# First RWKV layer's opening: two low-rank factors mixed ahead of the normed input, first weight splits issued in another place

## The reference

```python
h = rms_norm(x, norm_mix[0])
shifted = pad(h, one token)[:-1]
xm = h[:, :, None] + (shifted - h)[:, :, None] * mix      # six mixed inputs
r, k, v = xm[..., 0] @ w_r, xm[..., 1] @ w_k, xm[..., 2] @ w_v
logw = -softplus(-(w0 + tanh(xw @ w1) @ w2)) - 0.5        # xw = xm[..., 3], w1: 1024 x 64
decay = exp(-exp(logw))
a = sigmoid(a0 + (xa @ a1) @ a2)                          # xa = xm[..., 4], a1: 1024 x 64
g = sigmoid(xg @ g1) @ g2                                 # xg = xm[..., 5], g1: 1024 x 160
```

## Time and profile before

| | us |
|---|---|
| median of 3 runs | 1954.19 (1952.05 to 1954.6) |
| the profiled execution | 1962.87 |
| its span | 1960.7 |
| PE busy | 1834.4 (94%) |
| DVE busy | 1261.0 (64%) |
| ACT busy | 1043.6 (53%) |
| mean granted clock of PE | 0.967 |

### The profile page before, as it was taken

How to read it: one execution, slowest core, us unless ns; L and a number is a source line. 1 busy time by engine, 2 the same in 40 slices (tenths; PEclk the granted TensorE clock), 3 DMA queues, 4 the chain that set the end, 5 groups by cost and what they waited for, 6 DMA issues and landing times.

```text
span 1960.7 us, 43143 instructions
## 1 busy us (share of the span) xinstructions
PE 1834.4 (94%) x18559; PEld 1634.7 (83%) x18559; DVE 1261.0 (64%) x1783; ACT 1043.6 (53%) x1585; POOL 147.2 (8%) x106
## 2 busy tenths in 40 slices
PE   6988899999989999899899999988999999998998
PEld 5887798889869878888588888877788888887887
DVE  6865367865336666477657856777277766775764
ACT  5734455555455545355555555834455544565455
POOL 0061100000000000113100000052100000000000
PEclk8999999999989999999899999999999999998999
DMA  6320245557466655444646563320145555443541
GB/s 192 130 81 4 67 145 186 184 189 248 152 214 190 205 167 185 133 148 155 194 137 210 185 193 108 108 81 25 40 147 186 190 190 162 143 138 100 166 130 65
DMA packets 288532, 287.87 MB, mean 147 GB/s; under 512 B 15240, under 2 KB 286456, under 8 KB 288344
## 3 DMA queue, kind: packets, MB, share of 16 engines
q1 hardware_dynamic: 285048, 284.01, 45.4%
q10 hardware_dynamic: 3296, 1.11, 0.3%
HBM read 284.06 MB, written 1.05 MB: 145 GB/s over the span
## 4 chain that ended last, share of the span: by engine, by line
PE 89%; ACT 3%; DVE 3%; issue 3%; DMA 1%; POOL 0%; ACTq 0%; DVEq 0%; POOLq 0%
PE ps L419 22%; PE ps L420 12%; PE ps L401 10%; PE ps L402 9%; PE ps L403 9%; PE ps L814 3%; PE ps L436 2%; PE ps L437 2%; PE ps L438 2%; PE ps L712 1%; PE ps L784 1%; PE ps L675 1%; PE ps L798 1%; PE ps L641 1%; PE ps L676 1%
## 5 line engine op out<-in xcount | busy, mean ns | idle before, releaser
L463 DVE TENSOR_TENSOR wl<-raw,wh 128x1024 fp32r<-128x1024 f32 x484 | 597.2, 1252 | 366.0 <-ACT wh L453 361.7
L453 ACT ACTIVATE wh<-raw 128x1024 fp32r<-128x1024 f32 x484 | 499.5, 1041 | 452.8 <-PE ps L420 197.9
L419 PE MATMUL ps<-HH,wh 128*128 128x512 f32 x1408 | 491.2, 392 | 4.5 <-DVE mod L2143 4.5
L420 PE MATMUL ps<-HH,wl 128*128 128x256 f32 x1408 | 397.5, 282 | 0.0
L419 PEld LDWEIGHTS ps<-HH,wh 128*128 128x128 f32 x1408 | 265.0, 188 | 61.1 <-DVE mod L2143 4.8
L401 PE MATMUL ps<-HH,wh 128*128 128x256 f32 x928 | 272.8, 294 | 10.8 <-DVE HH L2511 5.7
L420 PEld LDWEIGHTS ps<-HH,wl 128*128 128x128 f32 x1408 | 266.7, 189 | 0.1
L402 PE MATMUL ps<-HH,wh 128*128 128x256 f32 x928 | 265.3, 286 | 0.0
L403 PE MATMUL ps<-HH,wl 128*128 128x256 f32 x928 | 265.1, 286 | 0.0
L401 PEld LDWEIGHTS ps<-HH,wh 128*128 128x128 f32 x928 | 181.0, 195 | 22.5 <-issue 6.8
L402 PEld LDWEIGHTS ps<-HH,wh 128*128 128x128 f32 x928 | 181.1, 195 | 1.3 <-issue 1.2
(11 more groups left out here) (324 smaller groups left out, 3138.3 us busy)
## 6 DMA issues: line engine op xcount, KB each, us to landing
raw<-in_ffn_w_gu_dram SPq DMA_DIRECT2D x88, 1024.0 KB, 5.1
raw<-in_ffn_w_down_dram SPq DMA_DIRECT2D x32, 1024.0 KB, 5.2
raw<-in_w_in_dram SPq DMA_DIRECT2D x32, 1024.0 KB, 5.5
raw<-in_rw_w_rkv_dram SPq DMA_DIRECT2D x24, 1024.0 KB, 5.6
B<-in_w_ada_dram SPq DMA_DIRECT2D x24, 1024.0 KB, 7.4
raw<-in_ds_w_in_dram SPq DMA_DIRECT2D x14, 1024.0 KB, 5.2
raw<-in_ffn_w_down_dram SPq DMA_DIRECT2D x16, 768.0 KB, 4.5
raw<-in_sb_w_qkv_dram SPq DMA_DIRECT2D x12, 1024.0 KB, 6.0
```

The source lines that it names most:

```text
L419: e.matmul(o[:, m, :], h_[:, k, c], x_, start=k0 + k == 0, stop=False, skip_group_check=True)
L420: i = e.matmul(o[:, m, 0:S], l_[:, k, c], x_[:, 0, :], start=False, stop=k0 + k == kt - 1, skip_group_check=True)
L453: e.activation(wh[:, u % UNITS, 0:kn * 256], raw[:, j % RAW, k0 * 256:(k0 + kn) * 256], ACT.Copy).then_inc(*up("hi"))
L463: e.tensor_tensor(wl[:, u % UNITS, 0:kn * 256], raw[:, j % RAW, k0 * 256:(k0 + kn) * 256], wh[:, u % UNITS, 0:kn * 256].bitcast(F32), ALU. ...
```

## The change

Four edits, all for the first RWKV layer alone (n == 0) but for the semaphore:

- The load of g1 gets a semaphore of its own, so that parts 3 and 4 wait for w1 and a1 alone.
- DVE mixes parts 3 and 4 before it waits for `rstd` and makes `h`; part 5 stays behind `h`.
- ACT makes `hi` of units 0 and 1 only, then waits for "wa" and takes tanh and copy, then does `prepare(1)`'s roundings, then `hi` of units 2 and 3, then `prepare(0)`'s.
- DVE makes `lo` of units 0 to 3 between `prepare(1)` and `prepare(0)`, and of units 4 and 5 ahead of the scan; the last `lo` before the fourth new key goes.

```diff
-            for name, a, z in (("rw_w1", 0, 64), ("rw_a1", 64, 128), ("rw_g1", 128, 256)):
-                e.dma_start(down[:, :, a:z], wview(A[name][n])[:, :, 0:z - a]).then_inc(s_down, 16)
+            for name, a, z, landed_ in (("rw_w1", 0, 64, s_down), ("rw_a1", 64, 128, s_down), ("rw_g1", 128, 256, s_down_g)):
+                e.dma_start(down[:, :, a:z], wview(A[name][n])[:, :, 0:z - a]).then_inc(landed_, 16)
...
-            hi(e, 2 if n else 4)
-            prepare(1, HH)
+            hi(e)
+            if n:
+                prepare(1, HH)
             e.wait_ge(*at("mm", ("wa", n)))
             e.activation(lor[0:64, :], PS("wa", n)[0:64, 0:S], ACT.Tanh)
             e.activation(lor[64:128, :], PS("wa", n)[64:128, 0:S], ACT.Copy).then_inc(*up("act", ("wa", n)))
+            if n == 0:
+                prepare(1, HH)
+                hi(e)
             prepare(0, XH)
...
-            e.wait_ge(s_down, 48 * (n + 1))
             for m in parts:
+                if m == 5:
+                    e.wait_ge(s_down_g, 16 * (n + 1))
+                else:
+                    e.wait_ge(s_down, 32 * (n + 1))
...
+            if n == 0:
+                dve_lora(e, 0, 3, 4)
             e.wait_ge(*at("act", (("rms w", n), "rstd")))
...
             if n == 0:
-                dve_lora(e, 0, 3, 4, 5)
+                dve_lora(e, 0, 5)
...
             prepare(1, (HH, HL))
+            if n == 0:
+                lo(e, 4)
             prepare(0, (XH, XL), ("dve", ("xml", n, 1, 3)))
-            lo(e, 2 if n else 4)
+            lo(e)
...
             if n == 0:
                 dve_lora_tail(e, 0)
                 dve_late_rows(e)
-            lo(e)
+            else:
+                lo(e)
             new_key(3)
```

More of the change, by code:

```diff
@@ L173, in build @@
         s_rows = [sem(f"s_rows{i}") for i in range(3)]
-        s_down, s_tail, s_lora_up, s_v2 = (sem(f"s_{n}") for n in ("down", "tail", "lora_up", "v2"))
+        s_down, s_down_g, s_tail, s_lora_up, s_v2 = (sem(f"s_{n}") for n in ("down", "down_g", "tail", "lora_up", "v2"))
         def C(name, a=0, b=None):
```

## The result

| | before | changed |
|---|---|---|
| median of 12 runs, us | 1960.36 (1952.05 to 1970.53) | 1968.37 (1960.55 to 1972.13) |
| ratio, 95% interval | | 1.0040 [1.0023, 1.0058] |
| profiled execution (span), us | 1962.87 (1960.7) | 1971.44 (1969.3) |
| granted clock, mean | 0.967 | 0.967 |
| chain of the span: PE, DVE, ACT | 89%, 3%, 3% | 86%, 5%, 4% |

The account below looks back on a forecast made before the run. PE was taken to bound the kernel, with little slack on DVE and ACT. Terms 2.65 + 2.5 + 2.7 = 7.9 us, taken as +8 on the median 1954.19, gave 1962.2 us; range 1956.5 to 1967.

Parts of the forecast that it names:

- the last line of the sum: Whole kernel: +8 us, giving 1970.9 against the profiled 1962.87, or 1962.2 against the median 1954.19.
- Part 1: DVE's factors ahead of h: they cost nothing in an idle gap, and PE begins "wa" 5.8 us earlier.
- Part 2: ACT waits for "wa" ahead of the roundings: first rounding into HH 1.67 us late, all of prepare(1) queued behind.
- my lower bound: Opening: the clock never falls, "wa" takes 6.9 us, the 1.67 us and the clock term vanish; +3.7 us.
- Part 3: Four `lo` between the inputs delay the sigmoid freeing "g"'s bank; PE's fourth w2/a2 group waits until 42.95: +2.65 us.
- Part 4: PE's clock after its 8.4 us stop: 0.50 for 5.1 us, until 48.0, delaying the first key unit: +2.5 us.
- Part 5: `lo` of units 4 and 5 ahead of DVE's scan: PE stands 2.7 us before the key's fourth block: +2.7 us.
- more clock loss: Rival: clock at 0.50 until 26.2 and again after the second stop; +12.4 us, 1966.6; chance 0.15.
- the early start: Rival: PE's opening starts 5.8 us earlier and nothing takes it back; 1948.4, faster; chance 0.05.
- the clock did cost: Judges the rival of no clock loss in PE's opening: +3.7 us, 1957.9; chance 0.15.
- later stops: Rival: PE's later stops, as the 2.4 us at 95.2, give it back; +1.3 us, 1955.5; chance 0.08.
- My upper bound: Opening: clock at 0.50 until 26.2, and 3.4 us more at 0.50 after the second stop; +12.4 us.

Follow-up runs that it names:

- e1: The kernel before with only the early mixing of w1's and a1's factors and g1's load on its own semaphore; 1965.70 us, ratio 1.0004.
- e7: The changed kernel with ACT's bank-freeing sigmoids ahead of XH's roundings, DVE's scan and rests ahead of prepare(0), factors mixed behind h again; 1968.86 us, ratio 1.0042.
- e2: The changed kernel with ACT's sigmoid of "g" moved ahead of the roundings into XH; 1967.21 us, ratio 1.0021.
- e3: The changed kernel with DVE's scan back ahead of the rests (`lo`) of units 4 and 5; 1968.05 us, ratio 1.0028.
- e6: The changed kernel with DVE's rests (`lo`) of units 0 to 3 back behind prepare(0); 1960.87 us, ratio 1.0000.
- e4: The changed kernel with PE repeating the third w2/a2 group's four matmuls nine times, 36 without use, to fill its stop; 1965.80 us, ratio 1.0017.

## Why the prediction was right or wrong

Measured against the kernel before beside it, the change costs 8.0 us; I had forecast 8. The time itself, 1968.37, lies outside my range (1956.5 to 1967). **The step that failed is the last line of the sum**, "against that median, 1954.19, it is 1962.2": the base was 6.2 us too low, because those three runs were low ones. Nine more runs of the same kernel brought its median to 1960.36, and the profiled execution, 1962.87, which I had set aside as "8.7 us above the median", was ordinary. The same sum on the median of the 12 runs gives 1968.4. Why the first three were low stays open: their clocks are not on record. In general the spread goes with the mean granted clock of the whole program. In the 35 runs of before beside e1, from 1954.06 to 1970.76 us at 0.972 and 0.965, the correlation of the two is -0.80; in the sets of 12 it lies between -0.58 (e7) and -0.94 (e2), at 0.7 to 2.6 us for each 0.001 of clock. That is a tie, and not shown to be the cause. My range held the unknown of the step, and not that of its base.

By the prediction's own steps:

- **Part 1**, nothing for the factors, "wa" 5.8 us earlier: right. It was 5.3 us, mostly since h started 0.45 us later in this execution (15.24 for 14.79). e1 shows it alone.
- **Part 2**, 1.67 us for ACT's wait ahead of the roundings: in the profiled execution nothing. The clock was not at half at the start, as in my lower bound, and "wa" ended before the roundings were ready. In e3, where the first matmuls ran at half pace, the fourth group came 1.5 us later, 0.3 of them from a later start of "wa": the term is there or not with the clock's state. The Trainium skill (TensorE: Matmul & The Clock Gate, "What's actually happening") has the gate's watching untied from the kernel, so that its changes fall differently from run to run; these two traces of the same opening agree, with tanh at 23.04 and at 24.78.
- **Part 3**, +2.65 for the bank of "g": the mechanism right to the row (a stop of 8.4 us forecast, 9.05 measured, released by L1535, at 42.95 forecast, 41.74 measured). The size was +1.44: the 1.67 of part 2 were not there, and from the start of `prepare(0)` to its last rounding it took 5.35 us (33.92 to 39.27) for my 4.94. e6 takes the four `lo` away and gets 4.70 us back; e2 shows the ring behind it.
- **Part 4**, +2.5 for the clock: 2.7 by e4, and 3.0 by the rows (the fourth block's +7.12 less 1.44 and 2.65). PE worked 6.1 us at 0.50 where I took 5.1 us. That it came so near is in part luck: in e3, behind a stop of 8.80 us, it was 3.2 us.
- **Part 5**, +2.7 for the scan: 2.65, gone in e3.
- **Behind part 5** came what I had only in the rival "more clock loss": the clock fell at the second stop too, and from the fourth block (+7.1) to the key norms (72.46 for 63.88, +8.6) another 1.5 us went.

So 1.44 + 3.0 + 2.65, and 1.5 behind them, is the 8.6 by the rows; with e4's 2.7 for the clock it is 8.3. The sum was right in part by luck: the bank's term was 1.2 us too large, and 1.5 us behind the fourth block were missing. The rivals' fate: the early start did not come through (e1), the clock did cost (e4), of "more clock loss" the part behind the second stop came and the one at the start did not, and later stops gave nothing back.

## What to carry to other kernels

An earlier start on the engine that bounds the kernel is worth only what the next bank's release allows: before moving work forward, walk the ring of banks and ask for each next owner which instruction frees it and what is queued ahead of that instruction. Work moved forward on one engine (four `lo` on DVE) delays everything it is moved ahead of; what mattered here was not DVE's own list but ACT's sigmoid and, behind it, PE's next bank. And a base of three runs can be nearly as far off (6.2 us) as the change is large (8.0 us): take the base's spread into the range.

## What the runs showed of the hardware

- Stops of the same length were followed by different clocks: 2.65 us ahead of 65.29 in the changed kernel by 0.50, but 2.67 us ahead of 62.59 in e4, 2.66 us ahead of 59.38 in e6 and 2.55 us ahead of 61.50 in e2 by 1.00. My upper bound had leaned on one such row.
- Through the clock, PE's stop of 9.05 us cost 2.7 us in addition to its own length, and 36 matmuls without use removed that part (e4).
- In the profile the clock's column can read 1.00 over an opening that runs at half pace: in e3 "wa" began at 1.19 us for two records, the pace of half clock in the earlier trace rows, under a column of 1.00 (16.1 to 17.5). There the durations tell, not the column.
